# Neighbourhood attention of a second block, from two grid rows against all 512 keys to 16 grid columns against 256 keys

## The reference, cut to what matters

```python
kr = min(NA_MAX_ROWS, rows)                      # 8 of 8 rows
col_start = np.clip(np.arange(GRID_W) - NA_COLS // 2, 0, GRID_W - NA_COLS)
col_idx = col_start[:, None] + np.arange(NA_COLS)[None, :]
s_w = jnp.einsum('bjhd,brjchd->bhjrc', q_i, k_w) * scale + bias[None]
s_c = jnp.einsum('bjhd,bnhd->bhjn', q_i, k_ctx) * scale
p = jax.nn.softmax(jnp.concatenate([s_w, s_c], axis=-1), axis=-1)
o = einsum(p_w, v_w) + einsum(p_ctx, v_ctx)
```

## Time and profile before

| | us |
|---|---|
| three runs | 4103.06, 4109.48, 4112.79; median 4109.48 |
| the profiled execution, its own time | 4102.35 |
| its span | 4101.1 |
| granted TensorE clock, mean over the span | 0.962 |
| PE busy | 3783.1 (92%) |
| DVE, ACT, POOL busy | 2245.6, 1499.0, 1133.2 |

### The profile page before, as it was taken

One profiled execution on the slowest core, in us unless ns is written; L12 is line 12 of the kernel. 1 busy time (PEld: TensorE's weight loads), 2 busy tenths in 40 slices (PEclk: granted clock), 3 DMA queues, 4 the chain that ended last, 5 costly groups with the idle time before them and its releaser, 6 DMA issues.

```text
span 4101.1 us, 54103 instructions
## 1 busy us (share of the span) xinstructions
PE 3783.1 (92%) x21364; PEld 3142.0 (77%) x21364; DVE 2245.6 (55%) x3735; ACT 1499.0 (37%) x2546; POOL 1133.2 (28%) x755
## 2 busy tenths in 40 slices
PE   5999899989998999798999799899999989899999
PEld 4888768788888888657888677678877867678777
DVE  6555684576656777645433689831156238840352
ACT  3223553443234323344322322442235223453352
POOL 1102204242015102204201423913221334525224
PEclk8999999999999999899999999899999999999999
DMA  7565324235654554303332311002110112113112
GB/s 265 175 199 158 124 75 157 91 130 185 227 179 133 186 194 160 100 31 109 127 99 83 122 48 55 33 27 72 49 49 12 65 49 77 48 36 106 60 37 93
DMA packets 131595, 433.12 MB, mean 106 GB/s; under 512 B 14480, under 2 KB 14480, under 8 KB 130704
## 3 DMA queue, kind: packets, MB, share of 16 engines
q1 hardware_dynamic: 130912, 427.04, 31.3%
q10 hardware_dynamic: 432, 2.62, 0.2%
HBM read 427.51 MB, written 2.10 MB: 105 GB/s over the span
## 4 chain that ended last, share of the span: by engine, by line
PE 73%; DVE 16%; issue 4%; ACT 4%; POOL 1%; DMA 1%; SPq 0%; DVEq 0%; ACTq 0%; POOLq 0%
PE ps L610 20%; PE ps L611 20%; PE ps L612 20%; DVE cut L2129 6%; PE ps L1847 2%; DVE cut L1033 1%; PE ps L1731 1%; PE ps L1814 1%; PE ps L1824 1%; ACT cut L528 1%; PE ps L608 1%; ACT cut L1869 1%; PE ps L636 1%; PE ps L637 1%; PE ps L638 1%
## 5 line engine op out<-in xcount | busy, mean ns | idle before, releaser
L610 PE MATMUL ps<-cut 128*128 128x512 f32 (+1 forms) x5216 | 1872.7, 359 | 160.3 <-DVE cut L538 45.7
L611 PE MATMUL ps<-cut 128*128 128x512 f32 (+1 forms) x5216 | 1835.2, 352 | 0.0
L612 PE MATMUL ps<-cut 128*128 128x512 f32 (+1 forms) x5216 | 1833.7, 352 | 0.0
L610 PEld LDWEIGHTS ps<-cut 128*128 128x128 f32 x5216 | 1012.4, 194 | 319.4 <-issue 99.2
L611 PEld LDWEIGHTS ps<-cut 128*128 128x128 f32 x5216 | 1014.0, 194 | 129.8 <-issue 4.8
L612 PEld LDWEIGHTS ps<-cut 128*128 128x128 f32 x5216 | 1012.1, 194 | 126.0
L538 POOL TENSOR_TENSOR cut<-cut 128x1024 fp32r<-128x1024 f32 (+3 forms) x304 | 671.1, 2211 | 1262.8 <-ACT cut L528 1262.2
L528 ACT ACTIVATE cut<-cut 128x1024 fp32r<-128x1024 f32 (+3 forms) x680 | 631.5, 936 | 532.5 <-PE ps L612 456.6
L538 DVE TENSOR_TENSOR cut<-cut 128x1024 fp32r<-128x1024 f32 (+3 forms) x376 | 447.8, 1193 | 458.6 <-ACT cut L528 458.5
L879 POOL TENSOR_TENSOR cut<-cut 128x512 fp32r<-128x512 f32 (+1 forms) x100 | 137.1, 1371 | 1011.2 <-ACT cut L839 1011.2
L2129 DVE SCALAR_TENSOR_TENSOR cut<-cut,cols 128x512 f32<-128x512 f32 (+1 forms) x330 | 280.4, 850 | 11.7
(11 more groups left out here) (293 smaller groups left out, 3901.3 us busy)
## 6 DMA issues: line engine op xcount, KB each, us to landing
cut<-in_ffn_in SPq DMA_DIRECT2D x200, 512.0 KB, 4.0
cut<-in_mod_w SPq DMA_DIRECT2D x128, 512.0 KB, 4.3
cut<-in_ffn_out SPq DMA_DIRECT2D x96, 384.0 KB, 3.2
cut<-in_ffn_out SPq DMA_DIRECT2D x96, 320.0 KB, 3.0
cut<-in_w_ada SPq DMA_DIRECT2D x48, 512.0 KB, 3.5
cut<-in_w_merge SPq DMA_DIRECT2D x48, 512.0 KB, 3.5
cut<-in_even_in SPq DMA_DIRECT2D x36, 512.0 KB, 3.6
cut<-in_proj SPq DMA_DIRECT2D x48, 256.0 KB, 2.6
```

Source lines behind the costliest of these rows:

```text
L610: te.matmul(o, hi[:, k - ka, w], xs[0], start=k == 0, stop=False)
L611: te.matmul(o, hi[:, k - ka, w], xs[1], start=False, stop=False)
L612: ins = te.matmul(o, lo[:, k - ka, w], xs[0], start=False, stop=last)
```

## The change

The 512 tokens are put in order of grid columns. An eighth is 8 columns in all 8 rows (64 tokens). Queries lie as eighths 0 to 7, so that a block of 128 queries is 16 columns; keys and values lie as tiles of two eighths: (0, 7), (1, 2), (3, 4), (5, 6). A block of queries meets tiles qb and qb + 1 (for the last: 3 and 0), 256 keys and not 512. Scores, bias, exponentials, transposes and the product with the values go over 256 + 256 positions; both heads' transposes share one bank and one eviction where the width is 256 (in the windowed attention too, for its blocks of 256 keys). The last block's score matmul is in two pieces of 128 keys. The tables become 1024 columns for each head, laid out for the four blocks.

The order is made by the evictions: ACT reads PSUM in runs of 8 numbers (`eighths`), and the gate `ngate` multiplies back into token order on DVE. Values are now made features first like the keys (four slabs of 128 columns, not two pairs of half slabs), evicted in column order into `VTR`, transposed by PE (6 per feature tile) and copied to `NV` by ACT (`values`). Groups 0 and 1 stand where the first half stood, group 2 and the transposes of 1 ahead of the keys' scaling, group 3 in attention step 0, transposes of 2 and 3 in steps 1 and 2. `ahead` has no special edge any more. In SP's queue the loads that belong to group 3 stand behind the first table.

```diff
-        edge = n if self.name[0] == "nv" and self.name[2] == 1 else last
...
-            return not plain and (SLABS[i].before is None or SLABS[i].before < edge)
+            return not plain and (SLABS[i].before is None or SLABS[i].before < last)
...
-        for g in range(2):
-            lin(("nv", l, g), "w2_nv", (l,), [g], mt=2, kch=4, low="g", toks=6)
+        lin(("nv", l), "w2_nv", (l,), range(4), low="g")
...
-    SBUFS = [region(Z0 + 1536 * i, 2, 768) for i in range(3)]
-    PBUFS = [region(Z0 + 1536 * i, 2, 768) for i in range(3, 5)]
+    SBUFS = {tag: [region(Z0 + 2 * w * i, 2, w) for i in range(3)] for tag, w in (("na", 512), ("wa", 640))}
+    PBUFS = {tag: [region(Z0 + 2 * w * i, 2, w) for i in range(3, 5)] for tag, w in (("na", 512), ("wa", 640))}
     Z1 = Z0 + 7680
-    tt_sb = [ar(Z1, Z1 + 1792), ar(13312, 13312 + 1792)]
+    tt_sb = [ar(Z0 + 5120, Z0 + 7168), ar(13312, 13312 + 2048)]
+    VTR = [ar(Z0 + 7168, Z0 + 7936), ar(Z0 + 7936, Z0 + 8704)]
...
-                    te.matmul(PS[b][:, 0:w], J["q"][s], J["k"][s], start=True, stop=True).then_inc(*sig("p_s", tag, i, s))
+                    for o, keys in J["k"][s]:
+                        ins = te.matmul(PS[b][:, o:o + keys.shape[-1]], J["q"][s], keys, start=True, stop=True)
+                    ins.then_inc(*sig("p_s", tag, i, s))
...
+                    o = 0
+                    if s and w == 256:
+                        b, o = bank["p_t", tag, i - 2, 0], 256
+                    else:
+                        b = yield from pe_take(("a_pt", tag, i - 2, 1 if w == 256 else s))
+                    bank["p_t", tag, i - 2, s] = b
                     for k in range(0, w, 128):
-                        ins = te.transpose(PS[b][:, k:k + 128], sbuf[:, s, k:k + 128], ident)
+                        ins = te.transpose(PS[b][:, o + k:o + k + 128], sbuf[:, s, k:k + 128], ident)
...
+                if w == 256:
+                    se.wait_ge(*(yield "p_t", tag, i - 2, 1))
+                    se.activation(pbuf[:, :, 0:w], PS[bank["p_t", tag, i - 2, 0]][:, :].rearrange("p (a n) -> p a n", a=2),
+                                  ACT.Copy).then_inc(*sig("a_pt", tag, i - 2, 1))
+                for s in range(2 if w > 256 else 0):
...
+    def eighths(x):
+        return x.rearrange("p (r o c) -> p o r c", r=8, o=8)
+
+    def two_eighths(t):
+        return slice(0, 8, 7) if t == 0 else slice(2 * t - 1, 2 * t + 1)
+
+    def in_eighths(x, n):
+        return x.rearrange("p (o r c) -> p o r c", o=n, r=8)
...
+                if tag == "ngate" and gi == 0:
+                    tb, x = tb.rearrange("p (r o c) -> p r o c", r=8, o=8), x.rearrange("p (o r c) -> p r o c", o=8, r=8)
+                ve.tensor_tensor(tb, x, tb, ALU.mult).then_inc(*sig("v_bp", tag, l, m, gi))
...
+                near = [(0, slice(qb * 128, qb * 128 + 256))] if qb < 3 else [(0, slice(384, 512)), (128, slice(0, 128))]
+                out.append(dict(w=256 if qb < 4 else 0, q=[NQ[r, t, q] for r in HEADS],
+                                k=[[(o, NK[r, t, n]) for o, n in near] for r in HEADS],
...
+                                mask=[table_at(l, t)[:, 1024 * s + 256 * qb:1024 * s + 256 * qb + 256] for s in range(2)] if qb < 4 else None,
...
+                                vready=[("a_nv", l, t, 1)] if qb == 0 else [],
+                                v=[[x[qb], x[(qb + 1) % 4]] + x[4:6] if qb < 4 else x[4:6] for x in vh], out=NQ[:, t, q]))
...
-        yield from pe_linear_tok(("nv", l, 0), nlhs, lambda t, c0: ("a_nv", l, 0, t), none)
+
+        def nv(*ms):
+            return pe_linear(("nv", l), nrhs, GR, lambda m, gi: ("a_vt", l, m, gi), none, ms=ms)
+
+        def values(m):
+
+            for i, ks in enumerate((range(4), range(4, 6))):
+                b = bank["p_vt", l, m, i] = yield from pe_take(("a_nv", l, m, i))
+                te.wait_ge(*(yield "a_vt", l, m, i))
+                for k in ks:
+                    ins = te.transpose(PS[b][:, 128 * (k % 4):128 * (k % 4) + 128], VTR[m % 2][:, 128 * k:128 * k + 128], ident)
+                ins.then_inc(*sig("p_vt", l, m, i))
+
+        yield from nv(0, 1)
+        yield from values(0)
         yield from pe_head_scale(("nq", l), QG, 0)
         yield from pe_head_sums(("nk", l), GR, 6)
 
-        def nv1(*ts):
-            return pe_tok_tiles(("nv", l, 1), nlhs, lambda t: ("a_nv", l, 1, t), ts)
-
         def agate(m):
             return pe_linear(("agate", l), nrhs, QG, lambda m, gi: ("a_ag", l, m, gi), none, ms=[m])
 
-        yield from nv1(0, 1)
+        yield from nv(2)
+        yield from values(1)
         yield from pe_head_scale(("nk", l), GR, 6)
-        yield from nv1(2)
...
-            0: lambda: nv1(3), 1: lambda: nv1(4), 2: lambda: nv1(5), n: lambda: agate(0), n + 1: lambda: agate(1)}))
+            0: lambda: nv(3), 1: lambda: values(2), 2: lambda: values(3), n: lambda: agate(0), n + 1: lambda: agate(1)}))
...
+                    if kind == "a_nk" and gi == 0:
+                        se.activation(in_eighths(x[:, 0:128], 2), eighths(p)[:, two_eighths(0)], fn).then_inc(*sig("a_nk0", l, m))
+                        x, p = in_eighths(x[:, 128:512], 6), eighths(p)[:, 1:7]
+                    if kind == "a_nq" and gi == 0:
+                        x, p = in_eighths(x, 8), eighths(p)
+                    se.activation(x, p, fn).then_inc(*sig(*key))
...
+        def nv(*ms):
+            def epilogue(m):
+                v = VTR[m % 2]
+                se.wait_ge(*(yield "p_mm", ("nv", l), m))
+                if m >= 2:
+                    se.wait_ge(*(yield "p_vt", l, m - 2, 1))
+                p = eighths(PS[bank[("nv", l), m, 0]][:, :])
+                se.activation(in_eighths(v[:, 0:128], 2), p[:, two_eighths(0)], ACT.Copy).then_inc(*sig("a_vt0", l, m))
+                se.activation(in_eighths(v[:, 128:512], 6), p[:, 1:7], ACT.Copy).then_inc(*sig("a_vt", l, m, 0))
+                se.activation(v[:, 512:768], PS[bank[("nv", l), m, 1]][:, 0:256], ACT.Copy).then_inc(*sig("a_vt", l, m, 1))
+            return act_linear(("nv", l), epilogue, ms)
+
+        def values(m):
+            for i, (k0, k1) in enumerate(((0, 4), (4, 6))):
+                se.wait_ge(*(yield "p_vt", l, m, i))
+                p = PS[bank["p_vt", l, m, i]][:, 0:128 * (k1 - k0)].rearrange("p (k n) -> p k n", n=128)
+                se.activation(NV[:, k0:k1, m * 128:(m + 1) * 128], p, ACT.Copy).then_inc(*sig("a_nv", l, m, i))
+
+        yield from nv(0, 1)
+        yield from values(0)
         yield from act_head_sums(("nk", l), NK, GR, 6)
-        yield from tok(("nv", l, 1), NV, 256, 256, ("a_nv", l, 1), (0, 1, 2))
-
-        def nv1(t):
-            return tok(("nv", l, 1), NV, 256, 256, ("a_nv", l, 1), (t,))
+        yield from nv(2)
+        yield from values(1)
...
-            0: lambda: nv1(3), 1: lambda: nv1(4), 2: lambda: nv1(5), 5: lambda: act_slabs(LIN["agate", l].ahead(0))}))
+            0: lambda: nv(3), 1: lambda: values(2), 2: lambda: values(3), 5: lambda: act_slabs(LIN["agate", l].ahead(0))}))
...
-        for name in (("nq", l), ("nk", l), ("nv", l, 0), ("nv", l, 1)):
+        for name in (("nq", l), ("nk", l), ("nv", l)):
...
-        for name in (("glu", l), ("nq", l), ("nk", l), ("nv", l, 0), ("nv", l, 1)):
+        for name in (("glu", l), ("nq", l), ("nk", l)):
             yield from sp_linear(name)
+        yield from sp_linear(("nv", l), (0, 1, 2))
...
+                sy.dma_start(table_at(l, t)[:, 1024 * s:1024 * (s + 1)], a["rpb"][l, 2 * t + s]).then_inc(*dsig(f"d_tt{s}{t % 2}", l, t))
+            if t == 0:
+                yield from sp_linear(("nv", l), (3,))
```

More of the change, by code:

```diff
@@ L504, in sp_rows, with sp_linear @@
             sy.dma_start(mring[:, j % MRING * D:(j % MRING + 1) * D], src).then_inc(*dsig(*row_of(j)))
-    def sp_linear(name):
+    def sp_linear(name, ms=None):
         L = LIN[name]
-        for m in range(1 if L.toks else L.groups):
+        for m in ms or range(1 if L.toks else L.groups):
             yield from sp_slabs(L.loads(m))
@@ L643, in pe_linear_tok @@
         at[("p_mm", name, "end")] = newest["p"]
-    def pe_tok_tiles(name, x, until, ts, ncol=256):
-        L = LIN[name]
-        for t in ts:
-            b = bank[name, t, 0] = yield from pe_take(until(t))
-            for i, (n, ka, kb) in enumerate(L.parts(0)):
-                if t == 0:
-                    yield from pe_weights(n)
-                hi, lo = [tiles(n, v) for v in halves(n)]
-                for k in range(ka, kb):
-                    xs = x(k, t)
-                    te.matmul(PS[b][:, 0:ncol], xs[0], hi[:, k - ka, :], start=k == 0, stop=False)
-                    te.matmul(PS[b][:, 0:ncol], xs[0], lo[:, k - ka, :], start=False, stop=False)
-                    ins = te.matmul(PS[b][:, 0:ncol], xs[1], hi[:, k - ka, :], start=False, stop=k == L.kt - 1)
-                if kb == L.kt:
-                    ins.then_inc(*sig("p_mm", name, t, 0))
-                elif t == L.toks - 1:
```

(30 more changed lines are left out.)

29 lines of the change are left out of this document (10 added, 19 removed).

## The result

Measured beside the kernel before on one chip: 4067.3 us, median of four executions (4064.4 to 4072.3), against 4108.6 (4103.1 to 4112.8). The ratio is 0.9902, 95% interval 0.9885 to 0.9919: 40 us shorter, 33 to 47. Two more sets gave 0.9901 (0.9884 to 0.9917) and 0.9905 (0.9891 to 0.9920). The forecast was 4075, its range 4060 to 4094. The profiled execution took 4064.73 us, its span is 4063.4 (before: 4102.35 and 4101.1).

What follows compares the result with a forecast made beforehand. PE bounds layer 1 from step 3; DVE bounds layer 0's first 65 us, then PE shares the chain with DVE and ACT. Layer 0 -15.1 and layer 1 -16.8 make -31.9 us; time put at 4075, range 4060 to 4094.

Steps and rivals of the forecast that it cites:

- The step of layer 1: Layer 1's attention from step 3, PE's groups alone: 4.63 us a step falls to 3.3, 1.33 saved.
- The tile of layer 0: Layer 0's attention after the taps: one feature tile falls from 24.8 us to 18.2, between 16.8 and 20.4.
- The start: PE's added values work ahead of the keys' scaling delays the stage by 3.4 us in layer 0, 3.3 in layer 1.
- The term that stays after the first steps: Later start and other early costs, less savings in the first steps: +1.9 us in each layer.
- The table's wait: DVE's 3.37 us wait for the first table, which grows from 448 to 512 KB a head: +0.2 us in each layer.
- POOL: POOL's first tap moves from 2544.41 to near 2569; net effect on DVE +0.8 us in layer 0, about the same in layer 1.
- rival 2: POOL's taps end last in layer 0 and delay the convolution's means: gain about 24 us, time 4083; chance 0.12.
- The low half: POOL's low half of the values, 2.4 us, now falls among DVE's taps: +2.0 us a layer.
- The first: Loop through DVE and ACT sets the pitch: tile 20.4 us, layer 1 step 3.7, gain 22, time 4084; chance 0.17.
- The fifth: No gain: a dependence of tables, `VTR` or banks stops steps in every tile; within 8 us of before; chance 0.04.
- The third: TensorE's clock falls because PE waits: a 3.3 us step takes 6.6, total +52 us, time 4159; chance 0.04.
- The fourth: More than forecast: 16.8 us a tile, 3.15 a step, cheaper group 2 at the start: -40 us, 4067; chance 0.08.

Runs made afterwards that it cites:

- e7: Changed kernel, but the two heads' transposed probabilities go to two PSUM banks and ACT evicts 256 columns twice instead of 512 once; ratio to the kernel before 0.9916.

## Why the prediction was right

**The step of layer 1** was forecast at 3.3 us and is 3.33, every group at its forecast price but the transposes (0.59 for 0.55). From the broadcast of the first step to that of the last, with the values behind it, the gain is 18.3 + 0.4 = 18.7 us, the number in the sum.

**The tile of layer 0** was forecast at 18.2 and is 17.6: from the ninth job on the stage gained 17.7 where the sum has 17.0. Taking the windowed attention and subtracting what this one lacks was better than PE's bare sum of 16.8, which isn't reached because of the loop at the context jobs. With the two heads' transposes evicted apart (e7) the tile takes 18.1 us between DVE's first maxima of it and of the next, against 17.5 in the changed kernel. So the merged eviction, which the forecast had not priced, makes up most of the 0.6.

**The start.** For the keys' scaling 3.4 us later was forecast in layer 0 and 3.3 in layer 1; 3.5 and 3.2 were measured in the first profile, but 2.3 in layer 0 in both others and 5.1 in layer 1 in one of them, by the accident of the clock. The term that stays after the first steps was 1.9 a layer (6 x 0.4 is 2.4 and not 2.5 in its sum), and measured 1.5 in layer 0 (first maximum of the ninth job) and 2.3 in layer 1. That the two misses cancel is luck. Undoing the values' new order gives 3.1 and 1.1 back, or 2.6 in layer 1 at a like clock. The table's wait was priced as it was before plus 0.2; it was 0.4 longer in layer 0. What I had not seen is that in layer 1 this old wait costs twice.

**POOL.** Its first tap came 25 us later, 24 by the stage's start, as forecast. Its last ended at 2684.26, 7.7 us ahead of the means, which were released by the gate's eviction: rival 2 is out. The low half was priced at 2.0 among DVE's taps. Eight taps took 6.2 to 6.6 us with it and 4.1 with POOL idle, which is about that, and in the wrong place it cost 1.9.

**Evictions in column order** cost nothing, and scores in two pieces 0.02 us, not 0.1.

**What was missed** is 2.3 us in layer 1 from the banks' turn. With the 0.7 of the tiles it makes up nearly all of the 3.1 between the forecast 31.9 and the measured 35.0 in the stages; the starts (0.4 less in layer 0, 0.4 more in layer 1) cancel. The forecast of 4075 lies 8 us above the median. Three of them are these; the other five are within what the medians tell (each ratio has 6 to 7 us to either side). All three sets put the gain at 39 to 41 us, though, and the stages at 33 to 35. Whether the difference is real, and where it would lie, no run shows.

**The rivals.** The first (the loop sets the pitch) is refuted in layer 1 by the doubled transposes and the added copy, and in layer 0 by the tile, 17.6 us for its 20.4. The fifth (no gain) is out by the stages. The third (clock) happened only where PE was not the bound: 0.68 in the first part of layer 0 (0.79 before) and 1.00 afterwards, and in layer 1 at the start and for a few microseconds behind the wait. The fourth had the time, 4067, but not its mechanism: the step is 3.33 and not 3.15, and the start is the forecast's. The tile of 17.6 lies between its 16.8 and the forecast's 18.2 and doesn't tell them apart.

## What to carry to other kernels

When an operation is narrowed, price the step of the engine that fills it from the nearest stage with that width, and check the other loop with a real stage of the same pattern, not with a sum. Ask of every wait of PE what clock it has afterwards: the wait and the slow work behind it come as a pair, so taking away a wait of under 3 us can be worth 5, as it was here. A change of the number of banks a step takes moves every later bank assignment, which can bring or take a wait of microseconds far from the change.

## What the runs showed of the hardware

- A 128x2 instruction on DVE took 2.02 us beside a 128x1024 subtraction on POOL and 0.17 without; it ended with POOL's. Eight taps on DVE took 4.05 to 4.13 us with POOL idle, 5.0 to 5.6 beside POOL's taps and 6.2 to 6.6 with the low half among them.
- The same idle stretch of PE in the same kernel was followed by a granted clock of 1.00 in one execution and 0.50 in another, 2.8 us apart. At the start of layer 1 it came back to 1.00 within the first microseconds in one (0.94 over the first eight) and not in the other (0.54), which moved the keys' scaling by 1.9 us. A single profile can't decide a difference of that size; the length of a stage, repeated and compared at a like clock, can.
- PSUM read in runs of eight numbers, 384 columns in 0.48 us and a group of queries (512 and 256 columns) in 0.87, goes at the speed of plain reads, which took 0.87 for the same group before.
